# Both block transfers of a mixture-of-experts loop issued from POOL: the result store moves off ScalarE's queue

## What is computed

```
g_p, g_idx = top 1 of softmax(t @ rg_w + rg_b)            # a group
e_p, e_idx = top 2 of the group's experts                  # two experts for each token
rows of a token are copied into a buffer sorted by expert, in padded blocks
y = (silu(x_block @ w_gate[e]) * (x_block @ w_up[e])) @ w_down[e]    # for each block
out[token] = sum over its two rows of weight * y
```

## Time and profile before

| | |
|---|---|
| median of 3 runs | 3503.95 us (3492.57 to 3511.65) |
| the profiled execution | 3507.12 us |
| its span, first to last instruction | 3505.5 us |
| busy: PE / DVE / ACT / POOL | 71% / 30% / 15% / 11% of the span |
| the three block loops, from the trace | 495 to 838, 1290 to 1867, 2865 to 3455 us: 1510 us together |
| DMA | 646 MB, of which 567 MB on SP's queue (weights) |
| mean granted TensorE clock | 0.831 |

### The profile page before, as it was taken

One profiled execution on the slowest core, in us unless ns is written; L12 is line 12 of the kernel. 1 busy time (PEld: TensorE's weight loads), 2 busy tenths in 40 slices (PEclk: granted clock), 3 DMA queues, 4 the chain that ended last, 5 costly groups with the idle time before them and its releaser, 6 DMA issues. The chain is left out here.

```text
span 3505.5 us, 74506 instructions
## 1 busy us (share of the span) xinstructions
PE 2491.8 (71%) x31542; PEld 1793.8 (51%) x31543; DVE 1037.5 (30%) x2767; ACT 520.8 (15%) x1257; POOL 370.8 (11%) x527
## 2 busy tenths in 40 slices
PE   8987957685998746754353897999998954556642
PEld 4465545464446445533242345989986443444431
DVE  0235321124008421210014303556555420111104
ACT  1133100011105000000001102323321010000000
POOL 0000110002000110000002001112113110000002
PEclk9998968797999868977686898888887877778876
DMA  5202159886110168999996100000002169998794
GB/s 203 86 28 109 61 197 325 327 318 231 54 72 25 45 234 311 337 355 386 368 364 238 44 24 1 1 0 0 0 0 82 73 231 378 359 345 327 273 387 179
DMA packets 101173, 646.48 MB, mean 184 GB/s; under 512 B 28690, under 2 KB 50450, under 8 KB 67300
## 3 DMA queue, kind: packets, MB, share of 16 engines
q1 hardware_dynamic: 41440, 567.30, 42.3%
q0 software_dynamic: 32896, 55.23, 4.9%
q10 hardware_dynamic: 26756, 22.82, 2.0%
HBM read 599.98 MB, written 45.09 MB: 184 GB/s over the span
## 5 line engine op out<-in xcount | busy, mean ns | idle before, releaser
L1165 PE MATMUL ps<-ring,arena 128*32 128x128 f32 x13440 | 414.4, 283 | 133.2 <-DVE arena L1208 89.8
L1174 PE MATMUL ps<-ring,arena 128*32 128x256 f32 x3360 | 266.4, 451 | 330.1 <-DVE arena L1223 325.3
L1165 PEld LDWEIGHTS ps<-ring,arena 128*32 128x32 f32 x13440 | 394.7, 115 | 171.7 <-issue 153.7
L1220 DVE TENSOR_TENSOR arena<-arena,ps 128x64 f32<-128x64 f32 x296 | 63.4, 214 | 977.0 <-ACT arena L1198 977.0
L1174 PEld LDWEIGHTS ps<-ring,arena 128*32 128x32 f32 x3360 | 118.8, 126 | 433.3 <-issue 369.9
L1198 ACT ACTIVATE arena<-ps 128x64 f32<-128x64 f32 x296 | 60.4, 223 | 1457.3 <-issue 831.6
L1174 PE MATMUL ps<-xt_mem,arena 128*32 128x256 f32 x1376 | 115.6, 478 | 191.9 <-DVE arena L1223 191.6
L1140 POOL DMA_DIRECT2D arena<-xybuf x148 | 100.5, 679 | 1400.6 <-DVE arena L1208 1354.7
L1165 PE MATMUL ps<-arena 128*32 128x128 f32 x5504 | 166.5, 279 | 18.6 <-issue 17.7
L1165 PEld LDWEIGHTS ps<-arena 128*32 128x32 f32 x5504 | 159.2, 113 | 34.1 <-issue 30.3
L1174 PEld LDWEIGHTS ps<-xt_mem,arena 128*32 128x32 f32 x1376 | 51.8, 132 | 236.9 <-issue 216.5
(11 more groups left out here) (385 smaller groups left out, 3838.5 us busy)
## 6 DMA issues: line engine op xcount, KB each, us to landing
ring<-in_experts SPq DMA_DIRECT2D x165, 2048.0 KB, 20.6
arena<-in_experts SPq DMA_DIRECT2D x50, 2048.0 KB, 22.2
xt_mem<-in_experts SPq DMA_DIRECT2D x25, 2048.0 KB, 24.2
ring<-in_mixer_chunks SPq DMA_DIRECT2D x24, 2048.0 KB, 12.4
xybuf<-arena ACTq DMA_DIRECT2D x160, 128.0 KB
arena<-xybuf POOLq DMA_DIRECT2D x160, 128.0 KB, 11.9
xybuf<-arena SPq DMA_DIRECT2D x1, 9216.0 KB, 25.6
rows<-in_ln_g POOLq DMA_DIRECT2D x6, 512.0 KB, 5.1
```

The lines of the kernel that those rows point to most:

```text
L1165: ins = pe.matmul(ps[at, 2 + half, 0:P], xg[:, k, :], w_gu[half][:, k, q, :], start=(k == 0), stop=(k == NK - 1))
L1174: ins = pe.matmul(ps[at, 4, 0:W], hT[:, f, :], w_d[:, f, q * W:(q + 1) * W], start=(f == 0), stop=(f == NT - 1))
L1220: dve.tensor_tensor(hidden[:, half, :], silu_g[:, half, :], ps[:, 2 + half, HALF:P], ALU.mult)\
```

## The change

- The store of block g-1's result is issued by POOL, not by ACT. ACT's loop holds only the waits for the gate/up halves and the two silus.
- POOL's loop now waits for `s_y` (the result of block g-1 is in `y_sb`), then issues the load of block g+3 and behind it the store of block g-1. Before, it waited for `s_xg` (block g's input has been transposed) and issued the load of block g+4. Three blocks are loaded ahead of the loop, not four.
- The three stores of spare rows ahead of the loop, and the last store and the waits for the stores behind it, move from ACT to POOL as well.

```diff
-                    for b in range(AHEAD):
+                    for b in range(AHEAD - 1):
                         pool.dma_start(x_in[:, b, :], rows_at(b)).then_inc(s_loaded[b], 16)
+                    for b in range(AHEAD - 1):
+                        pool.dma_start(spare_rows(b), y_sb[:, b, :]).then_inc(s_stored[b], 16)
                     with pool.Fori(0, fours) as p:
                         for b in range(AHEAD):
                             g = AHEAD * p + b
-                            pool.wait_ge(s_xg, g + 1)
-                            pool.dma_start(x_in[:, b, :], rows_at(g + AHEAD)).then_inc(s_loaded[b], 16)
+                            freed = (b - 1) % AHEAD
+                            pool.wait_ge(s_y, g + 1)
+                            pool.dma_start(x_in[:, freed, :], rows_at(g - 1 + AHEAD)).then_inc(s_loaded[freed], 16)
+                            pool.dma_start(rows_at(g - 1), y_sb[:, freed, :]).then_inc(s_stored[freed], 16)
+                    pool.wait_ge(s_y, AHEAD * fours + 1)
+                    pool.dma_start(rows_at(AHEAD * fours - 1), y_sb[:, AHEAD - 1, :]).then_inc(s_stored[AHEAD - 1], 16)
                     for b in range(AHEAD):
+                        pool.wait_ge(s_stored[b], fours * 16 + 16)
+                    for b in range(AHEAD - 1):
                         pool.wait_ge(s_loaded[b], fours * 16 + 16)
...
                 @block.scalar
                 def _(act):
-                    for b in range(AHEAD - 1):
-                        act.dma_start(spare_rows(b), y_sb[:, b, :]).then_inc(s_stored[b], 16)
                     fours = value(act, slice(E + 2, E + 3), high=MAXB // AHEAD)
                     with act.Fori(0, fours) as p:
                         act.preload_act_table(ACT.Silu)
                         for b in range(AHEAD):
                             g = AHEAD * p + b
-                            freed = (b - 1) % AHEAD
-                            act.wait_ge(s_y, g + 1)
-                            act.dma_start(rows_at(g - 1), y_sb[:, freed, :]).then_inc(s_stored[freed], 16)
                             for half in range(2):
                                 act.wait_ge(s_gu[half], g + 1)
                                 act.activation(silu_g[:, half, :], ps[:, 2 + half, 0:HALF], ACT.Silu).then_inc(s_silu[half], 1)
-                    act.wait_ge(s_y, AHEAD * fours + 1)
-                    act.dma_start(rows_at(AHEAD * fours - 1), y_sb[:, AHEAD - 1, :]).then_inc(s_stored[AHEAD - 1], 16)
-                    for b in range(AHEAD):
-                        act.wait_ge(s_stored[b], fours * 16 + 16)
                     act.activation(spot, eps_ln, ACT.Copy)
```

## The result

The changed kernel takes 3419.2 us (median of 4 runs, 3417.7 to 3425.1), the kernel before 3504.0. The ratio is 0.976 with a 95% interval of 0.973 to 0.979: faster by 2.4%, some 85 us. The forecast was 3528. The number is near that of the rival "free store", 3400.

What follows compares the result with a forecast made beforehand. Loops taken as nearer the weights' DMA time than PE's; with stores slowing weights, 350 + 591 + 591 = 1532 against 1510, +22 us, plus 3 for last stores: 3532 profiled, 3528 median; 8-in-10 range 3395 to 3590.

Steps and rivals of the forecast that it cites:

- free store: Rival, chance 0.20: a store in POOL's queue weighs on the weights as little as in ACT's; about 3400 us.
- A store there costs what a load costs: Block loops, POOL's queue: each store displaces weights like a load, 0.63 MB or 1.5 us of their time.
- The weights run at 325 GB/s throughout: Two larger loops: block traffic always in flight, so weights need 561 us plus 30 at ends and gaps, 591 each.
- I take 350: First loop: its time in us, chosen between 317 and 366, nearer the upper end.
- The pace of 13 us per block: Block loops: load and store behind each other in POOL's queue, 2 x 6.5 us per block while weights stream.
- At most this gives back the idle DMA time, 176 us: Three loops: upper limit of the gain from removing ACT's wait, 65 + 40 + 71 us of idle DMA time.
- ACT's wait, the issue and its 15 us: ACT's block loop: taken away by the change, so silus start with their gate/up half; silus waited 832 us for issue.
- unpacked-store rival: Rival, chance 0.07: POOL keeps 1 KB packets, a store holds its queue 18 to 20 us; about 3690 us.
- The later load: POOL's load of block g+3: hidden by its margin in calm stretches, late by some us in bursts, already counted.
- The wait put at zero: POOL's DMA issues: descriptor generation blocked while DVE holds the shared port pair; no row shows it, counted as zero.
- The small terms: POOL's two issues of 0.68 us and work ahead of the loops hidden; last store 1 us a loop, 3 in all.

Runs made afterwards that it cites:

- no_store: The changed kernel without the block loops' stores and the waits for them: 3339 us, ratio 0.955 to the kernel before.
- swap_whole: The kernel before with the queues exchanged: whole loads issued by ACT behind the silus, whole stores by POOL: 3485 us, ratio 0.997.
- quarter_store: The kernel before with ACT's store of a block cut into four DMAs of 32 partitions, still ahead of the silus: 3372 us, ratio 0.963.
- The lead alone: The kernel before with only POOL's load changed (waits for block g-1's result, loads block g+3), store still on ACT: 3506 us, ratio 1.003.
- quarter_pool: The changed kernel with load and store each cut into four DMAs of 32 partitions, all issued by POOL: 3340 us, ratio 0.956.

## Why the prediction was wrong

- **"A store there costs what a load costs", 1.5 us: wrong, and it decided the sign.** The step that failed is "Those small packets come with POOL's way of issuing, not with the direction of the transfer, so I take the upper end". The small packets did come, 144 packets in all as forecast. But they were not the price: with the same 144 packets the weights move 4.51 MB beside a store and 3.93 beside a load, and while a store is in flight the total is 415 GB/s, where the forecast had 345 to 360. Measured by the loops' budget, moving the store cost 15 us of DMA time, 0.10 us per block; leaving it out altogether gave 0.51 us per block, lateness included.
- **"The weights run at 325 GB/s throughout", 591 us for each of the larger loops: wrong by the same step.** They took 559 and 551 us, at 388 to 394 GB/s in total where load and store are both in flight. The sum of the free-store rival, 541 us, was 18 and 10 us low. It had the DMA engines busy for 511 of them and idle for 30; by their shares the two loops were busy for 542 and 529 us and idle for 17 and 22. Without stores (no_store) they are busy for 529 and 512, so the load's price was about right there, and what was missing is the store's small price in DMA time.
- **"I take 350" for the first loop: wrong, 328.** The rival's 325 is within 3 us of it. The pace of 13 us per block was to hold it; it may hold in part: the DMA share is still only 0.85, but no run shows what the rest waits for.
- **"At most this gives back the idle DMA time, 176 us": right.** Half of it, 88 us, came back, and this is the whole gain of the loops (88 less 15).
- **"ACT's wait, the issue and its 15 us" taken away: right as a reading, wrong as a cause.** In swap_whole no silu waits directly for an issue, and it takes as long as before; in quarter_store they stand behind the issue as before, and it gains 3.7%. The pace is the store's draining, 20 us beside the weights. The prediction read it in the earlier trace rows, 7 packets a us, and the forecast used that number for the unpacked-store rival only, not for what bounds before.
- **"The later load": half right.** The lead alone costs 9 us. The loads do come late behind the stores: DVE's wait for them grew from 71 to 331 us, where I counted it in a 13 us pace.
- **The wait put at zero** (POOL's issue held up by DVE): right. In the changed kernel the issues of load and store take 694 and 688 ns at the median and 703 at most.
- **The small terms** (issues, ends of the loops, last store) were too small to be checked here.
- **Range and chances.** The free store, 3400, had a chance of 0.20 and is the case that came, 19 us off; the range reached down to it. The Trainium skill's sentence quoted beside that rival (DMA: Bandwidth & Descriptors, "Issuing engines are not separate DMA queues"), that another issuer saves only issue time, gave the right number and not the reason: the issue time was back-pressure, and with another issuer the store became another set of packets, 4 KB in place of 1 KB, which drains three times as fast. In quarter_pool, too, it mattered who issued.

## What to carry to other kernels

A DMA issue that blocks for long is a symptom: find out how fast that queue drains beside the traffic that saturates the DMA engines, and compare this with the period of the work, before moving the issue elsewhere. Look at the shape of small transfers first. Cutting a 128 KB transfer into four so that its slowest dimension was 32 rows and not 4 brought 3.7% for the store and 6.4% for both, where moving the queue brought 2.4%; and with that done, load and store did better on two queues than on one (3277 against 3340, with a longer lead as well). When a transfer's price is carried over from another, the direction must be the same.

## What the runs showed of the hardware

- Beside weights that stream from HBM to SBUF, a 128 KB load through POOL's queue displaced 0.67 MB of them and a store with the same number, size and queue of packets 0.20 MB (medians of 30 and 29). In ACT's queue the total beside a load was 388 to 399 GB/s, beside a store 427 to 428.
- The same 128 KB store is 128 packets of 1 KB through ACT's queue and 32 packets of 4 KB (and 112 small ones) through POOL's; beside the weights the first drains in some 20 us, the second in some 6. A whole store adds 4 packets to its data in ACT's queue, a quarter of one 16.
- In four DMAs of 32 rows ACT's store lands after 11 us at the median (a whole one followed the one before at some 20), and POOL's load after 6.7 instead of 12.
- The DMA time that a second load took in the loops was 121 us, a second store's 47 us (1470 and 1396 us against 1349).
